# The S5 mixer of a two-block model rebuilt: five V products inside the first FFN, u and y turned by TensorE, y kept in PSUM with W stationary, the scan on one engine

## The chip, the cores and the metric

The kernel runs on one core of a Trainium2 chip. The metric is the device time of one execution in microseconds (us), as the median of several runs. A profiled execution of the same program gives the rows that are read below.

## What is computed

A model of 256 tokens and 1024 channels: a first block of four layers (mixers Fourier, S5, dilated attention, Fourier, each followed by a SwiGLU FFN) and a second block of two layers. Everything is float32. Only the S5 mixer, the mixer of layer 1, is touched. Cut to what matters, it is

```python
def _s5_direction(u, lam_re, lam_im, log_dt, b_re, b_im, c_re, c_im, reverse):
    lam = lax.complex(lam_re, lam_im)                    # 64 groups x 64 states
    dt = jnp.exp(log_dt)[:, None]
    lam_bar = jnp.exp(lam * dt)
    b_bar = ((lam_bar - 1.0) / lam)[..., None] * lax.complex(b_re, b_im)
    bu = lax.complex(einsum('bsgp,gnp->bsgn', u, b_bar.real),   # u: 256 tokens, 64 groups of 16 channels
                     einsum('bsgp,gnp->bsgn', u, b_bar.imag))
    # h[t] = lam_bar * h[t-1] + bu[t], forward or backward in time
    _, hs = lax.associative_scan(combine, (lam_bar, bu), axis=1, reverse=reverse)
    return einsum('gpn,bsgn->bsgp', lax.complex(c_re, c_im), hs).real

def s5_mixer(h, ...):
    y = (y_fwd + y_bwd).reshape(b, s, d) + d_skip * h
    g = jax.nn.gelu(y)
    val, gate = jnp.split(g @ w_glu, 2, axis=-1)
    return val * jax.nn.sigmoid(gate)
```

## The kernel before

The time axis of 256 tokens is cut into 32 chunks of 8 (S5_C = 32, S5_T = 8). The 64 groups are worked on in 8 tiles of 8 groups (f = 0..7). For each tile three factors are needed: **V** (powers of lam_bar times b_bar), which brings the inputs of a chunk into its state; **W** (powers of lam_bar times c), which brings the state carried into a chunk out to its 8 outputs; and a Toeplitz matrix of the **lags** inside a chunk. A V or a W is made elementwise by `s5_product`: 12 instructions of 128x512 elements on VectorE (DVE), or the same 12 on GpSimd (POOL).

Per tile, TensorE (PE) turns V (`factors`, 16 transposes), makes the lags from V and C (16 small matmuls), turns them (`toeplitz`, 8 transposes), applies V to u (L2049, "inputs", 32 matmuls into half of the output partitions each) and applies the Toeplitz matrix to u (L2057). ScalarE (ACT) copies each PSUM result out. V of tile 0 is made in the sixth chunk of the FFN before (`s5_first`); V of tiles 1 to 7 follow in the mixer, two buffers in turn.

u is wanted as rows (time in chunk, channel in group) by columns (tile, group, chunk), h is held as channels by tokens. Before, ACT permutes h (L957), ACT and POOL store it to DRAM in 8 DMAs (`s5_store_u`), and POOL loads it back in one. After the eight tiles the scan over 32 chunks runs as 30 steps of four dependent instructions, half of the columns on DVE (L1513 to L1518, 128x64), half on POOL (L790 to L793, 128x64). Then, per tile, PE multiplies the spread carried state (stationary) with W (moving) (`bring`, L2078), ACT copies the result (L1008), PE turns it back (`turn_back`, L2090), and DVE adds it to the y in SBUF (L1534). W of tiles 1 and 4 is made by POOL (`W_POOL`), the six others by DVE, four buffers in turn. y then takes the way of u through DRAM (`s5_store_y`, `s5_load_y`, two halves). Last come the skip term (L1541), GELU and the splitting into two float32r parts (L1023 to L1546), and the GLU projection of 8 weight panels (`project`, L1888 to L1890), each panel loaded by SP, split by ACT (L853) and DVE (L1324).

An FFN has 11 chunks of three weight panels each (`chunk`). PE's order in the FFN is fixed; DVE splits three panels per chunk (L1324) and makes the hidden activations (L1378 to L1393).

All engines run their own instruction list in order and meet through semaphores.

Of the kernel before, what the change touches and what calls it, by code (L numbers as in the profile page):

```python
# [12 lines left out]
P = 128  # L13
# [92 lines left out]
def build(nc, A, out, stop=None):  # L106
# [8 lines left out]
    with ExitStack() as ctx:  # L115
# [87 lines left out]
        s5_out_ready = sem("s5_out_ready")  # L203
        s5_y_ready = sem("s5_y_ready")
        s5_y_stored = {n: sem(f"s5_y_stored_{n}") for n in ("act0", "act1", "pool1")}
        s5_y_loaded = [sem(f"s5_y_loaded{i}") for i in range(2)]
        s5_cbd_ready = sem("s5_cbd_ready")
        s5_zbd_ready = sem("s5_zbd_ready")
        s5_wp_part = sem("s5_wp_part")
        s5_wp_ready = sem("s5_wp_ready")  # L210
        s5_skip_ready = sem("s5_skip_ready")
# [119 lines left out]
        s5.z = s5.take(2 * S5_G * S5_C).rearrange("p (r c k) -> p r c k", r=2, c=S5_G)  # L331
        s5.hperm = s5.z[:, 0].rearrange("p c k -> p (c k)").rearrange("p (f t c) -> p f t c", f=KT, t=S5_T)
        u_flat = s5.take(S5_G * S5_C)
        s5.u = u_flat.rearrange("p (g c) -> p g c", g=S5_G)
        s5.buf = [s5.take(2 * NC * P).rearrange("p (r c m) -> p r c m", r=2, c=NC) for _ in range(2)]
        win_flat = s5.take(2 * NC * P)
        s5.win = win_flat.rearrange("p (m q) -> p m q", m=2 * NC)
        b_flat = s5.take(2 * S5_G * S5_P)
        s5.b = b_flat.rearrange("p (r c m) -> p r c m", r=2, c=S5_G)
        s5.c = s5.take(2 * S5_G * S5_P).rearrange("p (r c m) -> p r c m", r=2, c=S5_G)  # L340
        s5.pow = s5.take(2 * (S5_T + 1) * S5_G).rearrange("p (r k c) -> p r k c", r=2, k=S5_T + 1)
        tmp_flat = s5.take(2 * NC * P)
        s5.tmp = tmp_flat[:, NC * P:].rearrange("p (r c m) -> p r c m", r=2, c=NC // 2)


        LAGS = 2 * S5_T - 1
        s5.kc = s5.take(LAGS * S5_P)

        s5.tc = rope[:, :, :].rearrange("p r s -> p (r s)").rearrange("p (g i m) -> p g i m", g=KT, i=S5_T)
        s5.rot = s5.take(2 * S5_G).rearrange("p (r c) -> p r c", r=2)  # L350
        s5.d = s5.take(KT)

        z_pool, z_dve = slice(0, S5_G // 2), slice(S5_G // 2, S5_G)
        s5.zp = s5.take(2 * S5_G).rearrange("p (i r c) -> p i r c", i=2, r=2)

        s5.back = [s5.take(2 * P)[0:2 * S5_C], s5.take(2 * P)[0:2 * S5_C], rstd[0:2 * S5_C, :]]
        s5_back_ready, s5_back_copied = s5_t_ready, s5_t_copied
        y_flat = hidden[:, :, :, :, :].rearrange("p a b t s -> p (a b t s)")
        s5.y = y_flat.rearrange("p (g c) -> p g c", g=S5_G)

        s5.w = s5.buf + [v.rearrange("p (r c m) -> p r c m", r=2, c=NC) for v in (win_flat, b_flat)]
        s5.wtmp = s5.tc.rearrange("p g i m -> p (g i m)").rearrange("p (r c m) -> p r c m", r=2, c=NC // 2)


# [2190 lines left out]
```

## Time and profile before

| what | us |
|---|---|
| median of 3 runs | 2757.31 (2755.21 to 2759.44) |
| profiled execution, its own time | 2759.11 |
| its span, first to last instruction | 2757.3 |
| PE busy over the span | 2598.0 (94%) |
| DVE busy | 1850.1 (67%) |
| ACT busy | 1265.1 (46%) |
| POOL busy | 308.6 (11%) |

The own time of the profiled execution is what compares with the median; its span leaves out what lies around the instructions. Stretches below are in us from the span's start. PE busy counts time, not pace; the clock in the rows is the granted TensorE clock as a share of full speed.

### The profile page before, as it was taken

The numbers are of one execution on the slowest core, as the hardware profiler recorded it, in microseconds if no ns is written. First come the engines' busy times: TensorE is split into PE (matmuls) and PEld (weight loads), VectorE is DVE, ScalarE is ACT, GpSimd is POOL, SyncE is SP. The second block draws the span as 40 slices with busy tenths as digits, with TensorE's granted clock in tenths as the row PEclk, the third lists the DMA queues.
The fourth block names the chain that finished last, engine by engine and source line by source line (L and its number), as shares of the span: only waits on it lengthen the run. The fifth ranks groups of instructions, "written<-read, shape, count | busy, mean of one in ns | idle before, by whom it ended". The sixth has DMA issues, their size and how long they took to land.

```text
span 2757.3 us, 51840 instructions
## 1 busy us (share of the span) xinstructions
PE 2598.0 (94%) x21706; PEld 2519.8 (91%) x21706; DVE 1850.1 (67%) x2303; ACT 1265.1 (46%) x1497; POOL 308.6 (11%) x419
## 2 busy tenths in 40 slices
PE   7997936999999999999999999999999999999998
PEld 7997835999899988999999999999999999999998
DVE  5765777655666575555657557986656656987655
ACT  5333413433455565334434334665434334665433
POOL 5400580000300010000000000230000000230000
PEclk9998967999999999999999999999999999999999
DMA  5554001555567773553554554444454554443553
GB/s 196 186 188 146 17 1 33 181 183 183 172 164 161 162 161 116 184 183 135 180 190 174 192 188 148 156 147 147 177 189 172 195 185 147 164 150 138 183 183 122
DMA packets 77781, 432.63 MB, mean 157 GB/s; under 512 B 20224, under 2 KB 23296, under 8 KB 27728
## 3 DMA queue, kind: packets, MB, share of 16 engines
q1 hardware_dynamic: 58720, 410.25, 41.4%
q0 software_dynamic: 5888, 17.53, 5.2%
q10 hardware_dynamic: 13040, 2.95, 0.6%
q8 instruction: 99, 1.62, 0.2%
q14 instruction: 34, 0.28, 0.0%
HBM read 426.40 MB, written 3.24 MB: 156 GB/s over the span
## 4 chain that ended last, share of the span: by engine, by line
PE 85%; DVE 8%; ACT 3%; POOL 1%; issue 1%; DMA 1%; ACTq 0%; DVEq 0%; POOLq 0%
PE psum L1888 25%; PE psum L1890 25%; PE psum L1889 25%; PE psum L2180 1%; DVE w_lo L1324 1%; PE psum L1921 1%; ACT w_hi L853 1%; PE psum L2156 1%; PE psum L2168 1%; PE psum L1990 1%; DVE arena L1513 1%; PE psum L2159 1%; DVE arena L1518 1%; DVE rstd L1349 1%; DVE h L1357 1%
## 5 line engine op out<-in xcount | busy, mean ns | idle before, releaser
L1888 PE MATMUL psum<-h_hi,w_hi 128*128 128x256 f32 x4320 | 1221.0, 283 | 32.4 <-DVE h_lo L1362 15.5
L1890 PE MATMUL psum<-h_hi,w_lo 128*128 128x256 f32 x4320 | 1211.5, 280 | 0.0
L1889 PE MATMUL psum<-h_lo,w_hi 128*128 128x256 f32 x4320 | 1211.2, 280 | 0.0
L853 ACT ACTIVATE w_hi<-raw 128x2048 fp32r<-128x2048 f32 x387 | 740.3, 1914 | 902.8 <-PE psum L1890 902.8
L1324 DVE TENSOR_TENSOR w_lo<-raw,w_hi 128x2048 fp32r<-128x2048 f32 x387 | 889.6, 2300 | 385.4 <-ACT w_hi L853 385.2
L1888 PEld LDWEIGHTS psum<-h_hi,w_hi 128*128 128x128 f32 x4320 | 815.1, 189 | 43.6 <-issue 35.7
L1889 PEld LDWEIGHTS psum<-h_lo,w_hi 128*128 128x128 f32 x4320 | 816.5, 189 | 1.2 <-issue 1.0
L1890 PEld LDWEIGHTS psum<-h_hi,w_lo 128*128 128x128 f32 x4320 | 815.5, 189 | 0.0
L1888 PE MATMUL psum<-act_hi,w_hi 128*128 128x256 f32 x1536 | 429.9, 280 | 1.7 <-DVE w_lo L1324 1.0
L1890 PE MATMUL psum<-act_hi,w_lo 128*128 128x256 f32 x1536 | 429.3, 280 | 0.0
L1889 PE MATMUL psum<-act_lo,w_hi 128*128 128x256 f32 x1536 | 429.1, 279 | 0.0
L1888 PEld LDWEIGHTS psum<-act_hi,w_hi 128*128 128x128 f32 x1536 | 288.0, 187 | 2.3 <-issue 1.2
L1889 PEld LDWEIGHTS psum<-act_lo,w_hi 128*128 128x128 f32 x1536 | 288.5, 188 | 0.0
L1890 PEld LDWEIGHTS psum<-act_hi,w_lo 128*128 128x128 f32 x1536 | 288.0, 187 | 0.0
L1386 DVE TENSOR_TENSOR hidden<-psum,rstd 128x512 f32<-128x512 f32 x88 | 60.8, 691 | 110.2 <-PE psum L1890 110.1
L1378 DVE TENSOR_TENSOR hidden<-psum,rstd 128x512 f32<-128x512 f32 x88 | 60.8, 691 | 103.6 <-PE psum L1890 103.3
L726 POOL DMA_DIRECT2D arena<-in_mix_col x2 | 1.2, 610 | 1106.4 <-DVE x L1423 1106.4
L1888 PE MATMUL psum<-w_hi,h_hi 128*128 128x256 f32 x320 | 92.2, 288 | 0.0
L1890 PE MATMUL psum<-w_hi,h_lo 128*128 128x256 f32 x320 | 89.7, 280 | 0.0
L1889 PE MATMUL psum<-w_lo,h_hi 128*128 128x256 f32 x320 | 89.4, 279 | 0.0
L2078 PE MATMUL psum<-arena 128*64 128x128 f32 x256 | 39.1, 319 | 51.5 <-DVE arena L1484 27.8
L1597 DVE SCALAR_TENSOR_TENSOR arena<-psum,arena 128x128 f32<-128x128 f32 (+1 forms) x96 | 32.0, 389 | 77.9 <-PE psum L2159 77.9
(313 smaller groups left out, 2689.7 us busy)
## 6 DMA issues: line engine op xcount, KB each, us to landing
raw<-in_panels SPq DMA_DIRECT2D x387, 1024.0 KB, 4.8
arena<-bias_by_distance POOLq DMA_DIRECT2D x32, 384.0 KB, 7.7
x<-in_x SPq DMA_DIRECT2D x1, 1024.0 KB, 7.4
arena<-in_s_b SPq DMA_DIRECT2D x1, 1024.0 KB, 15.0
arena<-in_s_c SPq DMA_DIRECT2D x1, 1024.0 KB, 16.5
arena<-s_u POOLq DMA_DIRECT2D x1, 1024.0 KB, 5.2
arena<-arena POOLq DMA_DIRECT2D x32, 32.0 KB, 1.9
out<-h SPq DMA_DIRECT2D x4, 256.0 KB, 2.2
```

Of the source, the lines that this page charges most:

```text
L853: a.activation(w_hi[:, s, :], raw[:, s, :], ACT.Copy).then_inc(hi_ready, 1)
L1324: v.tensor_tensor(w_lo[:, s, :], raw[:, s, :], w_hi[:, s, :].bitcast(F32), ALU.subtract).then_inc(lo_ready, 1)
L1349: v.reciprocal(rstd[:, :], rstd[:, :]).then_inc(rstd_ready, 1)
L1357: ins = v.scalar_tensor_tensor(h[:, c, :], x[:, c, :], gains[:, n * KT + c:n * KT + c + 1], rstd[:, :], ALU.mult, ALU.mult)
L1378: v.tensor_tensor(gate[:, c % 2], tiles(2 * c), rstd_2, ALU.mult).then_inc(scaled, 1)
L1386: v.tensor_tensor(act[:, b], tiles(2 * c + 1), rstd_2, ALU.mult).then_inc(scaled, 1)
L1513: v.tensor_tensor(m1, z0, l8, ALU.mult).then_inc(s5_step, 1)
L1597: ins = v.scalar_tensor_tensor(da.sc[:, u % 3, cols].rearrange("p (z j) -> p z j", j=P), da_bank(u)[:, cols].rearrange("p (z j) -> p z j", ...
L1888: t.matmul(o, w[0], xin[0], start=start, stop=False, skip_group_check=True)
L1889: t.matmul(o, w[0], xin[1], start=False, stop=False, skip_group_check=True)
L1890: return t.matmul(o, w[1], xin[0], start=False, stop=stop, skip_group_check=True)
L2078: last = t.matmul(bank[2 + n % 2][0:2 * S5_C, k * P:(k + 1) * P], s5.zbd[:, f % 2, r, 4 * d + pair, :], s5.w[f % 4][:, r, 4 * d + pair, :] ...
```

## The change

V of tiles 0 to 4 is made inside the FFN, a few instructions of it after each of its panels (8 per chunk from chunk 3 on, by a generator that `steps` draws from). The small block-diagonal form of C (`cbd`) is no longer made by POOL but computed on the host from the weights and loaded from HBM, 256 KB per tile. u is turned by PE: 128 matmuls of 32x32 tiles with a 0/1 matrix (`pick`) as weights, into PSUM, four copies out by ACT and DVE. The scan runs on DVE alone, all 128 columns in each instruction, and its tables and products lie in a PSUM bank. The Toeplitz product stays in PSUM, and the carried part is added to it there by PE, with W as the weights in 64x64 tiles and z moving (`carried`, 64 matmuls per tile of 31 columns). y is turned by 128 matmuls like those of u. POOL makes W of tiles 3, 4 and 5. The buffers are laid out anew: three of them are the slots of weight panels 37, 38 and 39, so that panels 39, 40 and 41 (the third, fourth and fifth of the GLU) are loaded only when the first carried tile, the last carried tile, and the turning of y are done. The order of the lag matmuls changes so that four neighbours write to four different column strips.

The diff, cut to its core:

```diff
-        W_POOL = (1, 4)
+        S5_EARLY = 5
+        W_POOL = (3, 4, 5)
+        W_DVE = (0, 1, 2, 6, 7)
+        W_ORDER = (0, 1, 2, 3, 4, 6, 5, 7)
+        def s5_bank(n):
+            return bank[4 + (n + 1) % 4]
+        def s5_y_bank(f, e):
+            return bank[f // 4 * 2 + e]
...
+                for n in range(s5_n0 + 2, s5_n0 + 5):
+                    sp.wait_ge(lo_ready, n - SLOTS + 1)
+                    if n == s5_n0 + 2:
+                        sp.wait_ge(s5_out_ready, W_ORDER.index(0) + 1)
+                    if n == s5_n0 + 3:
+                        sp.wait_ge(s5_out_ready, W_ORDER.index(7) + 1)
+                    if n == s5_n0 + 4:
+                        sp.wait_ge(s5_y_ready, 2)
+                    sp.dma_start(raw[:, n % SLOTS, :], A["panels"][n]).then_inc(panel_loaded[n % SLOTS], 16)
...
             def s5_mixer(st):      # GpSimd
+                for f in range(1, KT):
+                    if f >= 2:
+                        pool.wait_ge(s5_fill, s5_use("K", f - 2) + 1)
+                    pool.dma_start(s5.cbd[f % 2], A["s5_cbd"][f].rearrange("p (r c n) -> p r c n", r=2, c=NC)
+                                   ).then_inc(s5_cbd_loaded[f % 2], 16)
+                pool.wait_ge(s5_fill, s5_use("I", KT - 1) + 1)
...
                     split(p + 2, i, 6)
+                    steps(ahead, 3)
                     scale_gate(c, p, i)
                     split(p + 3, i, 6)
+                    steps(ahead, 2)
                     hidden(c, p, i)
                     split(p + 4, i, 6)
+                    steps(ahead, 3)
...
             def s5_mixer(st):      # VectorE
+                due = s5_v(5)
+                steps(due, 6)
+                v.wait_ge(s5_u_ready, 2)
+                for b in (1, 3):
+                    v.tensor_copy(s5.u[:, b].rearrange("p g f c -> p (g f c)"), bank[b][:, :]).then_inc(s5_u_copied, 1)
+                steps(due)
+                steps(s5_w(0))
+                for f in (6, 7):
+                    v.wait_ge(s5_fill, s5_use("K", f - 4) + 1)
+                    steps(s5_v(f))
+                for f, k in ((1, 4), (2, 5), (6, 6)):
+                    v.wait_ge(s5_fill, s5_use("K", k) + 1)
+                    steps(s5_w(f))
+                v.wait_ge(s5_evac, 64)
+                tabs = bank[5][:, 0:7 * S5_G].rearrange("p (i c) -> p i c", i=7)
                 for k in range(1, S5_C - 1):
-                    z0, z1 = s5.z[:, :, z_dve, k - 1], s5.z[:, :, z_dve, k]
+                    z0, z1 = s5.z[:, :, :, k - 1], s5.z[:, :, :, k]
...
+                steps(s5_w(7))
...
             def s5_mixer(st):      # TensorE
+                def rows_of_u(v):
+                    for g in range(2):
+                        for k in range(2):
+                            for b in range(4):
+                                rows = slice(b * 32, (b + 1) * 32)
+                                for tb in range(4):
+                                    i = S5_T - 1 - (2 * tb + k)
+                                    at = g * S + v * P
+                                    last = t.matmul(bank[b][tb * 32:(tb + 1) * 32, at:at + P],
+                                                    s5.pick[rows, g, (1 - k) * S5_P:(3 - k) * S5_P],
+                                                    h[rows, 4 * v:4 * v + 4, i::S5_T],
+                                                    start=(v + g + k == 0), stop=(v + g + k == 3), skip_group_check=True)
+                    last.then_inc(s5_u_ready, 1)
+                for f in range(KT):
+                    within(f)
+                    inputs(f)
+                    if f + 1 < KT:
+                        toeplitz(f + 1)
+                    if f + 2 < KT:
+                        factors(f + 2)
+                        lags(f + 2)
+                t.wait_ge(s5_step, 2 + 4 * (S5_C - 2))
+                for n, f in enumerate(W_ORDER):
+                    carried(f)
+                    if n == 5:
+                        channels_of_y(0)
+                channels_of_y(1)
```

Where the instructions go, at the three places that matter. First DVE in the FFN before the mixer, one chunk of its list. Here w_lo is the low part of a split panel, hidden the gate and up tiles, arena and rope the places of V and its temporaries. Before:

```order
L1324 TENSOR_TENSOR w_lo<-raw,w_hi 128x2048 [waits hi_ready] x2
L1378 TENSOR_TENSOR hidden<-psum,rstd 128x512 [waits panel_done]
L1324 TENSOR_TENSOR w_lo<-raw,w_hi 128x2048 [waits hi_ready]
L1386 TENSOR_TENSOR hidden<-psum,rstd 128x512 [waits panel_done]
L1389 TENSOR_TENSOR hidden<-hidden 128x512 [waits gate_ready,scaled]
```

And now, in chunks 3 to 10:

```order
L1271 TENSOR_TENSOR w_lo<-raw,w_hi 128x2048 [waits hi_ready]
L1434 TENSOR_TENSOR arena<-arena 128x512
L1436 TENSOR_TENSOR rope<-arena 128x512
L1438 TENSOR_TENSOR rope<-arena 128x512
L1325 TENSOR_TENSOR hidden<-psum,rstd 128x512 [waits panel_done]
L1271 TENSOR_TENSOR w_lo<-raw,w_hi 128x2048 [waits hi_ready]
L1441 TENSOR_TENSOR arena<-arena,rope 128x512 [waits s5_v_part]
L1443 TENSOR_TENSOR arena<-arena,rope 128x512
L1333 TENSOR_TENSOR hidden<-psum,rstd 128x512 [waits panel_done]
```

Up to three instructions of a product now stand between the split of a panel and the instruction that waits for PE.

Second, DVE's scan, one step of it before (the last row is the first of the next step):

```order
L1513 TENSOR_TENSOR arena<-arena 128x64 [waits s5_step]
L1514 TENSOR_TENSOR arena<-arena 128x64
L1516 TENSOR_TENSOR arena<-arena 128x2x32 [waits s5_step]
L1518 TENSOR_TENSOR arena<-arena 128x2x32 [waits s5_step]
L1513 TENSOR_TENSOR arena<-arena 128x64 [waits s5_step]
```

and now, with the two copies that fill the tables ahead of it:

```order
L1490 COPY psum<-arena 128x64 [waits s5_evac]
L1491 COPY psum<-arena 128x128
L1498 TENSOR_TENSOR psum<-arena,psum 128x128 [waits s5_step]
L1499 TENSOR_TENSOR psum<-arena,psum 128x128
L1501 TENSOR_TENSOR arena<-arena,psum 128x128 [waits s5_step]
L1503 TENSOR_TENSOR arena<-arena,psum 128x128 [waits s5_step]
```

The width doubles, and each instruction has one operand in PSUM where all were in SBUF.

Third, PE behind the scan. Before, one tile of eight (two halves, each brought out and turned back; arena holds the spread state, W and the copies):

```order
L2078 MATMUL psum<-arena 64x128 [waits s5_t_copied,s5_zbd_ready,s5_w_ready]
L2078 MATMUL psum<-arena 64x128 x7
L2090 MATMUL psum<-ident,arena 128x64 [waits s5_t_copied]
L2090 MATMUL psum<-ident,arena 128x64
L2078 MATMUL psum<-arena 64x128 [waits s5_t_copied]
```

Now two tiles of eight:

```order
L2063 MATMUL psum<-arena,raw 64x31 [waits s5_w_ready,s5_step]
L2063 MATMUL psum<-arena,raw 64x31 x63
L2063 MATMUL psum<-arena 64x31 [waits s5_w_ready]
L2063 MATMUL psum<-arena 64x31 x63
L2063 MATMUL psum<-arena 64x31 [waits s5_wp_ready]
```

Where a tile had 16 matmuls, two copies by ACT and four short matmuls, it now has 64 matmuls of 31 columns, one wait, and no copy between.

## Rows read from the trace of the kernel before

**Rows 1.** Busy us (count) of PE, PEld, DVE, ACT, POOL; clock, DMA share, GB/s.

```profile
216.00:250.40 34.40, 34.40 (x295) 34.40 (x294) 19.74 (x18) 14.33 (x11) 0.00 (x0) 1.00 0.53 183
250.40:280.60 30.20, 11.82 (x76) 9.42 (x74) 18.02 (x27) 11.00 (x20) 5.68 (x8) 0.66 0.46 105
280.60:362.90 82.30, 72.87 (x1032) 65.38 (x1032) 56.95 (x86) 32.77 (x64) 53.60 (x105) 0.94 0.01 2
362.90:422.40 59.50, 12.76 (x71) 11.64 (x70) 57.39 (x128) 6.68 (x17) 41.43 (x62) 0.61 0.00 0
422.40:460.70 38.30, 30.67 (x218) 26.73 (x218) 32.45 (x55) 12.27 (x32) 0.00 (x0) 0.89 0.11 14
460.70:480.70 20.00, 9.62 (x51) 9.32 (x51) 10.06 (x14) 8.70 (x15) 2.67 (x4) 0.66 0.35 79
```

**Rows 2.** The chain of waits, 255 to 283 us: start, us, what.

```profile
270.49 4.30 DMA s_u<-arena
...
275.36 5.17 DMA arena<-s_u
```

**Rows 3.** Timeline of PE, most of one of the eight tiles.

```profile
303.12 1.15 PE L2009 MATMUL psum<-ident,arena 128*128 128x128 f32 x8 [0.25 <-ACT arena L967]
304.19 2.46 PE L2021 MATMUL psum<-arena 128*32 128x128 f32 x32
306.58 1.97 PE L2057 MATMUL psum<-arena,rope 128*128 128x32 f32 x16
...
309.39 2.06 PE L2049 MATMUL psum<-arena 128*64 128x32 f32 x64
```

**Rows 4.** Timeline of DVE, the scan: first beside POOL, then alone.

```profile
386.40 1.11 DVE L1513 TENSOR_TENSOR arena<-arena 128x64 f32<-128x64 f32 x1
...
390.77 1.26 DVE L1513 TENSOR_TENSOR arena<-arena 128x64 f32<-128x64 f32 x1
...
393.77 0.26 DVE L1513 TENSOR_TENSOR arena<-arena 128x64 f32<-128x64 f32 x1
...
394.12 0.26 DVE L1516 TENSOR_TENSOR arena<-arena 128x64 f32<-128x64 f32 x1
394.41 0.27 DVE L1518 TENSOR_TENSOR arena<-arena 128x64 f32<-128x64 f32 x1
```

**Rows 5.** Timeline of POOL, a W product beside that scan.

```profile
383.76 1.26 POOL L812 TENSOR_TENSOR arena<-arena,rope 128x512 f32<-128x512 f32 x1
```

**Rows 6.** Timeline of PE, half a tile brought out.

```profile
434.91 1.96 PE L2078 MATMUL psum<-arena 128*64 128x128 f32 x16
```

**Rows 7.** Timeline of DVE, part of a chunk of the FFN.

```profile
216.65 0.69 DVE L1378 TENSOR_TENSOR hidden<-psum,rstd 128x512 f32<-128x512 f32 x1 [1.41 <-PE psum L1890]
218.59 2.29 DVE L1324 TENSOR_TENSOR w_lo<-raw,w_hi 128x2048 fp32r<-128x2048 f32 x1 [1.25 <-ACT w_hi L853]
...
229.90 2.29 DVE L1324 TENSOR_TENSOR w_lo<-raw,w_hi 128x2048 fp32r<-128x2048 f32 x1 [2.79 <-ACT w_hi L853]
```

**Rows 8.** Timeline of PE, the sums of the norm ahead of the mixer.

```profile
250.37 3.62 PE L1921 MATMUL psum<-h,ones 128*128 128x256 f32 x16
```

**Rows 9.** Timeline of DVE, the eight instructions that make h.

```profile
256.38 3.25 DVE L1357 SCALAR_TENSOR_TENSOR h<-x,gains,rstd 128x256 f32<-128x256 f32 x8
```

**Rows 10.** Timeline of DVE, instructions with one operand in PSUM.

```profile
29.15 0.29 DVE L1456 TENSOR_TENSOR h<-h,psum 128x127 f32<-128x127 f32 x1 [1.89 <-ACT h L923]
29.36 0.28 DVE L1457 TENSOR_TENSOR h<-h,psum 128x127 f32<-128x127 f32 x1
...
45.48 0.68 DVE L1438 TENSOR_TENSOR x<-psum,x 128x512 f32<-128x512 f32 x1
```

**Rows 11.** Timeline of POOL at the same time.

```profile
45.67 0.60 POOL L669 TENSOR_TENSOR arena<-arena 128x64 f32<-128x64 f32 x2
```

**Rows 12.** The page, DMA issues: KB of each, median us from issue to landing.

```profile
raw<-in_panels SPq DMA_DIRECT2D x387, 1024.0 KB, 4.8
...
x<-in_x SPq DMA_DIRECT2D x1, 1024.0 KB, 7.4
```

More of the change, by code:

```diff
@@ L329, in take @@
                 return arena[:, cls.at - n:cls.at]
[L331 to L337, printed above, removed]
@@ L356, in build @@
[L356 to L362, printed above, removed]
@@ new lines, in toeplitz, with inputs @@
+                def toeplitz(f):
+                    t.wait_ge(s5_evac, s5_use("K", f) + 1)
+                    for q in range(2):
+                        to = take(s5_use("C", f) + q)
+                        for i in range(4):
+                            last = t.transpose(to[:, i * P:(i + 1) * P],
+                                               s5.kc[:, (4 * q + i) * S5_P:(4 * q + i) * S5_P + P], ident[:, :])
+                        last.then_inc(s5_fill, 1)
+                def inputs(f):
+                    t.wait_ge(s5_evac, s5_use("T", f) + 4)
+                    to = take(s5_use("I", f))
@@ L2053, in s5_mixer @@
-                    t.wait_ge(s5_t_copied, 2 * f + 2)
-                    if f:
-                        t.wait_ge(s5_intra_copied, f)
-                    for g in range(KT):
-                        last = t.matmul(bank[1][:, g * S5_C:(g + 1) * S5_C], s5.tc[:, g].rearrange("p i m -> p (i m)"),
-                                        s5.u[:, f * KT + g, :], start=True, stop=True)
-                    last.then_inc(s5_intra_ready, 1)
-                w_dve = [f for f in range(KT) if f not in W_POOL]
@@ L2095, in s5_mixer @@
-                for n in range(2 * KT):
-                    bring(n)
-                    if n:
-                        turn_back(n - 1)
-                turn_back(2 * KT - 1)
+                                rhs = s5.u[:, c % 4, e, f, :] if c < 4 else s5.u[:, c % 4, e, f, ::-1]
+                                last = t.matmul(to[half[e], (r * NC + c) * S5_C:(r * NC + c + 1) * S5_C],
+                                                s5.win[f % 2][:, r * NC + c, half[e]], rhs, start=True, stop=True)
@@ new lines, in s5_mixer @@
+                factors(0)
+                lags(0)
+                toeplitz(0)
+                factors(1)
+                lags(1)
+                t.wait_ge(s5_loaded, 64)
+                for v in range(2):
+                    t.wait_ge(h_ready, 4 * st["whole"] + 2 * v + 2)
+                    rows_of_u(v)
+                t.wait_ge(s5_u_copied, 4)
+                for f in range(KT):
+                    within(f)
+                    inputs(f)
+                    if f + 1 < KT:
+                        toeplitz(f + 1)
+                    if f + 2 < KT:
+                        factors(f + 2)
+                        lags(f + 2)
```

508 lines of the change are left out of this document (231 added, 277 removed).

## The prediction

> **What bounds the kernel now.** I read the page first, then the busy time by stretch, then the chain of waits and the timelines inside the mixer. Outside the mixer PE runs nearly without a gap, so the change can only win or lose inside it and in the FFN ahead. In the mixer no single engine bounds; four stretches follow one another [rows 1]. From 250.4 to 280.6 us (30.2 us) PE is busy 11.8 us: the norm, then u on its way through DRAM, whose last two legs alone are 4.30 and 5.17 us [rows 2]. From 280.6 to 362.9 (82.3 us) PE is busy 72.9 us and sets the pace in most tiles: V turned, lags, Toeplitz, inputs [rows 3]. From 362.9 to 422.4 (59.5 us) PE has 12.8 us of work at a mean clock of 0.61 and waits for the scan and the first W products; DVE is busy 57.4. From 422.4 to 460.7 (38.3 us) DVE's W products pace PE. From 460.7 to 480.7 (20.0 us) y goes through DRAM and PE does the first GLU panel, much of it at the slow clock (mean 0.66). The FFN before them passes 295 matmuls in 34.4 us, 0.117 us each at full clock.
>
> The scan deserves a look [rows 4]. Alone, a step of four DVE instructions takes 0.94 us (393.77 to 394.41, plus 0.30 for the last). Beside POOL's W products it takes 4.37 us (386.40 to 390.77): each DVE instruction lasts 1.11 to 1.26 us, and a POOL instruction beside them 1.26 [rows 5]. DVE's instructions there have two inputs in SBUF.
>
> **The change part by part.** I carry the new clock along, from 250.4, and compare at the same events.
>
> *V in the FFN.* Four more products of 12 instructions of 128x512, at 0.69 us each (the row of such an instruction [rows 7]), are 4 x 12 x 0.69 = 33 us of DVE. In a chunk DVE idles 1.41, 1.25 and 2.79 us at three of its waits [rows 7]; a fourth is like the first. The eight instructions per chunk (5.5 us) go in as three, two and three. Three are 2.1 us against 1.41: the gate product starts 0.7 us late. What is late next is ACT's silu, which stands behind ACT's split of the next panel, and DVE waits 1.25 us for that split anyway, so the 0.7 us ends there. Price 0; with that cover gone, 0.7 us in each of eight chunks, 5 us; at the very most all 33 us.
>
> *The start of the mixer.* The norm's sums end at 250.4 + 3.6 = 254.0 [rows 8]. PE then turns V0 and V1, makes two sets of lags and one Toeplitz without waiting for h: transposes 4 x 1.15 + 1.1 us, lags 2 x 1.0 (below), so 7.8 us with a stop for a copy: 261.8. h is complete at 259.6 [rows 9]. Turning u is 128 matmuls, each two records in the trace. Inputs at 32 columns in two column strips pass at 2.06/64 = 32 ns, start to start 31 ns per record [rows 3]. A 128-column record in one strip alone is 1.96/16 = 122 ns, less its tail 109 [rows 6]. With four strips in turn I take 31 ns, the smallest spacing any row shows: 256 x 31 = 8.0 us. Bounds: a quarter of 109, 27 ns, is 7 us; no overlap, 109 ns, is 28 us. Then 1.4 us of copies by two engines: the tile loop begins at 271.2 where it began at 280.6. **Minus 9.4.**
>
> *The tile loop.* Inputs 2.0, within-chunk 1.9, transposes 2.1 and 0.9 stay. Lags, 32 records in 2.4 us, 75 ns each where one strip is used eight times running [rows 3], now go round four strips: 31 ns, 1.0 us. Bound: unchanged 2.4, which is 8 x 1.4 = 11 us more in all. Six rounds of 8.1, and 9.7 for the last two tiles with one wait for a copy: 58.3 us. DVE has V5, V6, V7 and W0, W1, W2, W6 to make, 6.5 x 12 x 0.69 = 54 us from 271 on (half of V5 is made earlier), done with the loop's last tile, some 4 us before its end; POOL no longer spreads C (PE waited 7.7 us for that). The loads of C, 256 KB each, start two rounds ahead. With the last copy the scan starts at 330.3.
>
> *The scan.* 30 steps of 128 columns. PSUM instructions of 127 columns last 0.28 to 0.29 us and follow each other at 0.21 [rows 10]. A step is two at 0.21 to 0.25 and two dependent ones at 0.32 to 0.37 (duration plus the 0.03 to 0.04 that the lone scan shows [rows 4]): 1.06 to 1.24 us, I take 1.12. 33.6 us plus 0.7 for the tables: **364.6**. This supposes that POOL no longer holds DVE up, though it makes W3, W4, W5 just then (12 instructions of 1.1 to 1.26 us [rows 4, 5], 13.8 us each, 41 us). For it: at 45.48 a DVE instruction with one input in PSUM took its usual 0.68 us while POOL worked from 45.67 on [rows 10, 11]. That is one instruction beside narrow POOL ones. The Trainium skill, "SBUF — State Buffer", section on who interferes with whom, makes it a rule: a DVE instruction with at most one SBUF input does not contend with GpSimd, one with two does. By it the scan is the same 33.6 us. If it did contend, nine steps of 4.37 would pass in 41 us and 21 more of 1.12: 63 us, 30 more. Loop and scan together: 93.4 us where 82.3 + 59.5 = 141.8 stood. **Minus 48.4.**
>
> *Out of the scan.* PE sat idle over 30 us, so it starts at the 1.2 GHz level (clock 0.5); in the last stretch before, 51 matmuls were busy 9.6 us where 0.117 each makes 6.0, 3.6 us lost over two starts [rows 1]; I take 2.1 for one. Carried: 8 x 128 records x 31 ns = 32 us. Bounds: two of these 64x64 tiles at a time is what the 31 ns shows; four at a time would be 15.5 ns, 16 us; one at a time 58 ns (two at a time is 2 x 29), 59 us. I take the row. Turning y: 8 us, as for u (7 to 28). Copies between: 0.9. 43.0 us against 38.3: y is turned at 407.6. **Plus 4.7.** Before, such a tile took two halves of 1.96 us plus the turning back, about 4.4 us [rows 6], mostly hidden behind DVE; now 4.0 of PE. The Trainium skill, "TensorE: Matmul & The Clock Gate", section "Wait — 56ns, not 53.3ns?", says that matmuls never start closer than about 25 ns however few columns they have, which speaks against W as weights with 31 columns moving: more and smaller matmuls gain nothing. An estimate by it: 8 x 128 x 25 ns = 25.6 us for the carried part, 6 us under my row; it rules out the 16.
>
> W3 and W4 are due when three and four tiles are done, W5 as the seventh; POOL has them at about 343, 357 and 371. W7 follows the scan on DVE, 8 to 10 us. No wait.
>
> *The end.* One DVE round of additions 1.5 us, the low part of b = 0 another 0.7, then 48 matmuls of 0.117, 5.6 us at full clock, GELU of the second half hidden behind the first parts: 7.9 us against 20.0. **Minus 12.1.** Panels 39, 40, 41 are waited for by SP: 39 is free early, 40 after the last carried tile, 41 after the turning; a panel lands 4.8 us after issue [rows 12], and they are wanted 14 us and more behind the turning. Nothing late.
>
> *The start of the kernel.* 256 KB more beside the 1024 KB of x, which lands after 7.4 us [rows 12]: at most a quarter of that, 1.9 us, if it all shared x's way; it is issued after three loads on another queue, so I take 0.5.
>
> **The sum.** -9.4 - 48.4 + 4.7 - 12.1 + 0.5 = -64.7. The profiled execution took 2759.1 us in all (span 2757.3), the median is 2757.3; both lose the same, so 2757.3 - 64.7 = **2692.6 us**.
>
> **The rivals.**
> - *PE is faster in tiles.* 16 to 26 us carried, lags and turning at 27 ns: 8 to 18 us less, 2675 to 2685. For it: four disjoint tiles follow each other. Against: no row shows it.
> - *POOL still stops the scan*: plus 30, 2723. For it: the 4.37 us steps. Against: [rows 10, 11].
> - *PE's tiles overlap only in part*: the 32x32 turns at 60 to 109 ns (plus 15 to 40), or carried at 58 ns (plus 27): 2706 to 2745. For it: h is read with a stride of 8 elements, which no row shows.
> - *The FFN is held up* by the products, which are not hidden: up to plus 33, 2726.
> - *Slower than before: no overlap at all.* Turns plus 20 each, lags plus 11, carried plus 27: plus 78, 2771, 0.5% slower. It decides from 65 us on, that is when the mean record costs about 85% of these surcharges. Against: the inputs' 31 ns in two strips is overlap.
> - *The change does not do what it says*: the stall of the scan only moves behind W3 to W5. It would need POOL to take 20 us per product; it takes 13.8.
>
> **How the numbers follow.** Forecast (2685 to 2706) 0.5; faster PE 0.2; partial overlap 0.13; POOL contention 0.06; FFN held up 0.05; no overlap 0.03; something that eats the gain 0.03. The range reaches over the faster case's middle and most of the partial ones: 2670 to 2728. A measurement of this kernel tells 0.2% (5.5 us) from no change. Faster 0.95, same 0.01, slower 0.04.
>
> **What would show it.** In the changed profile: the FFN's chunks still 17 us and PE without gaps there; u turned in 8 us from about 262; rounds of 8 us with lags of 1.0; scan steps of 1.12 us that do not change when POOL ends; records of the carried part 31 ns apart; 8 us from the last turn to the end of the first GLU panel. I am wrong if scan steps are over 2 us, if 128 turning matmuls take over 15 us, or if PE waits for w_lo in the FFN.

## The result, and the profile after

The changed kernel takes 2696.53 us (median of four runs, 2688.91 to 2698.23), the kernel before on the same chips 2756.26 us: a ratio of 0.9776, 95% interval 0.9755 to 0.9797, 60 us less. The prediction said 2692.6 us, 2670 to 2728.

The profiled execution took 2698.23 us (span 2696.4) where that of before took 2759.11: 60.9 us less, against 64.7 predicted. Busy time by stretch answers to [rows 1], in the same columns (PE, PEld, DVE, ACT, POOL, clock, DMA):

```profile
214.00:248.00 34.00, 34.00 (x291) 34.00 (x290) 25.81 (x28) 14.42 (x11) 0.00 (x0) 1.00 0.34 121
251.50:266.30 14.80, 12.49 (x360) 9.71 (x358) 10.03 (x18) 7.38 (x15) 1.10 (x2) 1.00 0.14 39
266.30:328.50 62.20, 60.38 (x984) 57.13 (x984) 49.57 (x80) 27.11 (x54) 3.15 (x5) 0.90 0.07 19
328.50:370.80 42.30, 0.00 (x0) 0.00 (x0) 40.23 (x121) 4.26 (x9) 39.79 (x36) 0.50 0.00 0
370.80:408.80 38.00, 34.83 (x1280) 32.30 (x1280) 10.51 (x17) 3.98 (x7) 0.00 (x0) 0.50 0.17 54
408.80:420.50 11.70, 8.78 (x51) 8.81 (x52) 7.04 (x9) 4.22 (x6) 0.00 (x0) 0.61 0.41 147
```

The FFN's stretch has PE busy all 34.00 us, five products or one; busy time says nothing of pace, but 291 matmuls in 34.0 us is the pace of before (295 in 34.4). From the end of the norm's sums to the start of the 48th matmul of the first GLU panel it is 168.6 us where it was 226.3. The third stretch ends with the scan's first step: all of the scan, 42.3 us, lies bare, with PE idle. The last three stretches run at half clock or little more.

The timeline of PE, from the norm's sums into the tile loop, answers to [rows 8] and [rows 3]:

```profile
251.33 1.91 PE L1991 MATMUL psum<-ident,arena 128*128 128x128 f32 x16
253.17 1.08 PE L2003 MATMUL psum<-arena 128*32 128x128 f32 x32
...
258.52 3.92 PE L2045 MATMUL psum<-h,arena 32*32 32x128 f32 x174
262.81 2.04 PE L2045 MATMUL psum<-h,arena 32*32 32x128 f32 x82 [0.37 <-issue]
266.33 2.38 PE L2033 MATMUL psum<-raw,hidden 128*128 128x32 f32 x16 [1.48 <-DVE raw L1474]
268.65 3.63 PE L2024 MATMUL psum<-raw,arena 128*64 128x32 f32 x64
272.21 1.97 PE L2013 MATMUL psum<-ident,arena 128*128 128x128 f32 x8
...
277.11 1.97 PE L2033 MATMUL psum<-raw,hidden 128*128 128x32 f32 x16
279.01 2.06 PE L2024 MATMUL psum<-raw 128*64 128x32 f32 x64
281.00 1.09 PE L2013 MATMUL psum<-ident,arena 128*128 128x128 f32 x8
```

Lags take 1.08 us where they took 2.46. Turning u is the 256 records of L2045: 6.3 us, 25 ns each. Behind it stands one wait, 1.48 us for the copy. A round is 7.67 us (277.11 to 284.78); the first has the same instructions longer, at the slow clock.

The scan answers to [rows 4], and POOL beside it to [rows 5]:

```profile
356.71 0.38 DVE L1498 TENSOR_TENSOR psum<-arena,psum 128x128 f32<-128x128 f32 x1
357.00 0.37 DVE L1499 TENSOR_TENSOR psum<-arena,psum 128x128 f32<-128x128 f32 x1
357.28 0.38 DVE L1501 TENSOR_TENSOR arena<-arena,psum 128x128 f32<-128x128 f32 x1
357.70 0.40 DVE L1503 TENSOR_TENSOR arena<-arena,psum 128x128 f32<-128x128 f32 x1
358.13 0.38 DVE L1498 TENSOR_TENSOR psum<-arena,psum 128x128 f32<-128x128 f32 x1
```

```profile
357.46 1.11 POOL L781 TENSOR_TENSOR hidden<-arena 128x512 f32<-128x512 f32 x1
```

A step is 358.13 - 356.71 = 1.42 us with POOL at work right beside it; all 30, before and after POOL's last instruction at 369 us, take 42.3.

PE behind the scan, and into the first GLU panel:

```profile
370.85 3.64 PE L2063 MATMUL psum<-arena,raw 64*64 64x31 f32 x128 [43.40 <-DVE arena L1503]
374.28 5.53 PE L2063 MATMUL psum<-arena 64*64 64x31 f32 x199
381.21 12.38 PE L2063 MATMUL psum<-arena 64*64 64x31 f32 x441 [1.40 <-issue]
393.53 3.54 PE L2077 MATMUL psum<-raw,arena 32*32 32x128 f32 x128
...
405.89 2.82 PE L2077 MATMUL psum<-raw,arena 32*32 32x128 f32 x128 [0.81 <-DVE raw L1511]
411.72 0.55 PE L1865 MATMUL psum<-h_hi,w_hi 128*128 128x256 f32 x1 [3.01 <-DVE h_lo L1523]
412.07 0.41 PE L1866 MATMUL psum<-h_lo,w_hi 128*128 128x256 f32 x1
412.29 0.41 PE L1867 MATMUL psum<-h_hi,w_lo 128*128 128x256 f32 x1
```

Carried records stand 12.38/441 = 28 ns apart, at the slow clock, with pauses marked "issue", in which PE waits for nothing that the profile shows (1.40 us). Behind the last turning PE idles 3.01 us for h's low part, and the panel starts at 0.21 us a matmul.

### The profile page after: what moved, and what is told of

Read it like the earlier page. It is cut to its first block, busy times and chain, and to the rows that moved or that the text cites. A ratio compares the mean times of both kernels' runs of the same rounds, so it can differ in the third digit from the quotient of the medians.

```text
span 2696.4 us, 54054 instructions
## 1 busy us (share of the span) xinstructions
PE 2579.1 (96%) x22954; PEld 2507.2 (93%) x22954; DVE 1822.7 (68%) x2288; ACT 1242.6 (46%) x1442; POOL 241.6 (9%) x276
## 4 chain that ended last, share of the span: by engine, by line
PE 90%; DVE 6%; ACT 2%; issue 1%; DMA 0%; DVEq 0%; ACTq 0%
PE psum L1865 26%; PE psum L1866 26%; PE psum L1867 25%; PE psum L2187 1%; PE psum L2063 1%; DVE w_lo L1271 1%; PE psum L1898 1%; ACT w_hi L818 1%; PE psum L2163 1%; PE psum L2175 1%; PE psum L2024 1%; PE psum L1967 1%; PE psum L2033 1%; PE psum L1991 1%; PE psum L2166 1%
## 5 line engine op out<-in xcount | busy, mean ns | idle before, releaser
L1865 PE MATMUL psum<-h_hi,w_hi 128*128 128x256 f32 x4320 | 1220.7, 283 | 24.7 <-DVE h_lo L1309 14.9
L1098 ACT ACTIVATE arena<-psum 128x512 f32<-128x512 f32 x48 | 28.6, 597 | 96.2 <-PE psum L1867 95.9
## 6 DMA issues: line engine op xcount, KB each, us to landing
arena<-in_s_b SPq DMA_DIRECT2D x1, 1024.0 KB, 15.4
```

The costliest lines, as they stand in the source:

```text
L1098: a.activation(dst, halves(landed(p)), func).then_inc(mix_copied, 1)
L1865: t.matmul(o, w[0], xin[0], start=start, stop=False, skip_group_check=True)
```

## The experiments

All start from the changed kernel unless said otherwise; changed_again is that kernel unedited, run beside shared_early. Times are medians (two_tiles_in_turn ran once); ratios are to the kernel before on the same chip. The table reads each profile's PE timeline: "sums" is where the norm's sums end, then come the stretches in us: to the start of the tile loop; from there to the first carried record (loop and scan); to the last turning; to the start of the 48th matmul of the first GLU panel; and their sum.

| kernel | median | sums | start | loop, scan | out | end | sum |
|---|---|---|---|---|---|---|---|
| changed | 2696.5 | 251.5 | 14.8 | 104.5 | 37.9 | 11.4 | 168.6 |
| changed_again | 2697.7 | 251.4 | 15.4 | 105.1 | 38.0 | 10.9 | 169.3 |
| scan_in_sbuf | 2722.8 | 252.7 | 15.5 | 130.0 | 39.0 | 10.1 | 194.6 |
| w_all_dve | 2700.7 | 251.4 | 15.3 | 105.2 | 38.2 | 10.5 | 169.2 |
| early_one | 2723.6 | 246.6 | 41.7 | 105.8 | 37.2 | 11.3 | 196.0 |
| same_tile_runs | 2734.4 | 244.6 | 42.3 | 115.2 | 37.4 | 10.9 | 205.8 |
| two_tiles_in_turn | 2715.2 | 251.4 | 24.6 | 105.7 | 38.2 | 10.9 | 179.5 |
| warm_pe | 2699.1 | 250.9 | 15.4 | 105.9 | 35.3 | 8.9 | 165.5 |
| early_lo | 2695.9 | 245.3 | 15.5 | 105.6 | 38.3 | 7.3 | 166.7 |
| shared_scan | 2691.3 | 253.3 | 15.5 | 94.3 | 38.6 | 11.0 | 159.3 |
| shared_early | 2679.8 | 245.0 | 15.5 | 93.5 | 39.0 | 7.4 | 155.5 |
| shared_early_warm | 2685.6 | 244.3 | 15.4 | 95.1 | 35.8 | 7.3 | 153.6 |

The sums end anywhere from 244.3 to 253.3 us with the same instructions ahead of them (early_one's apart): some executions passed the dense matmuls of the first FFN almost 3% faster (1092 in the 125 us from 120 in early_lo, 1064 in the changed kernel and in the kernel before), all at a granted clock of 1.00. So a difference of 3 us is read from the stretch, not from the median.

**Does the scan's place free it from POOL?** scan_in_sbuf puts the tables and products back into SBUF:

```
-tabs = bank[5][:, 0:7 * S5_G].rearrange(...)
+tabs = hidden_flat[:, 1024:1024 + 7 * S5_G].rearrange(...)
```

> The changed kernel with one line moved: the scan's tables and products lie in SBUF instead of a PSUM bank, so that every scan instruction has two SBUF inputs again, beside the same POOL products. Theory 1 (the operands' place is what freed the scan from POOL): beside POOL's 36 instructions DVE instructions wait for POOL's as in the kernel before (1.11 to 1.26 us each, 4.37 us a step), so nine or ten steps pass in POOL's 41 us, and the other 20 at 1.2 to 1.4 us: the scan takes 41 + 26 = 67 us instead of 42.3, the kernel about 25 us more than the changed one, 2721 us. Theory 2 (POOL and DVE did not meet because of timing or width, not because of the place): the scan takes 42 us or less, and the kernel 2690 to 2697 us.

2722.8 us, ratio 0.988 (0.9847 to 0.9912): 26 us more than the changed kernel. The timelines of DVE and of POOL, in the scan:

```profile
345.37 1.19 DVE L1499 TENSOR_TENSOR hidden<-arena,hidden 128x128 f32<-128x128 f32 x1
346.48 0.38 DVE L1501 TENSOR_TENSOR arena<-arena,hidden 128x128 f32<-128x128 f32 x1
346.89 1.27 DVE L1503 TENSOR_TENSOR arena<-arena,hidden 128x128 f32<-128x128 f32 x1
```

```profile
345.25 1.15 POOL L782 TENSOR_TENSOR hidden<-arena 128x512 f32<-128x512 f32 x1
346.48 1.44 POOL L784 TENSOR_TENSOR arena<-arena,hidden 128x512 f32<-128x512 f32 x1
```

From 330 to 371 us DVE got 44 instructions through, from 371 to 398 us 76. The scan took 69.7 us (theory 1 said 67). Theory 2 falls. The rule of the Trainium skill, "SBUF — State Buffer", section "Who interferes with whom", holds here: two SBUF inputs contend, one does not.

**The same part alone in the kernel before.** before_psum_scan moves only DVE's half of the scan (64 columns) to PSUM:

```
-l8, rot = s5.pow[:, 0, S5_T, z_dve]..., s5.rot[:, :, z_dve]
-m1, m2 = (tmp_flat[:, i * S5_G:(i + 1) * S5_G]...)
+tabs = bank[0][:, 0:7 * S5_G // 2]...  # copies of both tables, m1, m2
```

> The kernel before with one part of the change alone: DVE's half of the scan (64 columns) keeps its tables and products in a PSUM bank. POOL's half of the scan and its W products stay. Theory 1: no step waits for POOL any more; 30 steps of 0.94 to 1.1 us from 361.7 us on end at about 393 instead of 414.7 us. Of these 21 us PE gets back what the later W products don't take: 12 to 20 us, the kernel 2757 - 15 = 2742 us. Theory 2: POOL's instructions hold up the scan wherever its operands lie; no change, 2757 us.

2747.78 us, ratio 0.9951 (0.9932 to 0.9969): 13.5 us less by the ratio, 12.4 by the medians. The scan's steps are 0.93 us and it ends at 389.97 us; in the kernel before DVE's first product behind it starts at 414.71:

```profile
414.71 0.69 DVE L1478 TENSOR_TENSOR arena<-arena 128x512 f32<-128x512 f32 x1
```

The scan ends 24.7 us earlier, then, but only about half of it arrives. Here is where the rest went, DVE's next products and POOL's W4 beside them:

```profile
402.42 1.48 DVE L1478 TENSOR_TENSOR arena<-arena 128x512 f32<-128x512 f32 x1
403.82 1.74 DVE L1479 TENSOR_TENSOR arena<-arena 128x512 f32<-128x512 f32 x1
405.49 1.75 DVE L1480 TENSOR_TENSOR arena<-arena 128x512 f32<-128x512 f32 x1
```

```profile
398.79 1.55 POOL L808 TENSOR_TENSOR arena<-arena 128x512 f32<-128x512 f32 x1
```

Products with two SBUF inputs now meet POOL's: 1.5 to 1.75 us each instead of 0.69, and POOL's 1.4 to 1.7 instead of 1.1 to 1.3. The stall moved one stage on.

**What a step costs by itself.** w_all_dve has the scan in SBUF and POOL silent:

```
-W_POOL = (3, 4, 5)
-W_ORDER = (0, 1, 2, 3, 4, 6, 5, 7)
+W_POOL = ()
+W_ORDER = (0, 1, 2, 6, 3, 7, 4, 5)  # DVE makes 3, 7, 4, 5 behind the scan
...
-tabs = bank[5][:, 0:7 * S5_G].rearrange(...)
+tabs = hidden_flat[:, 1024:1024 + 7 * S5_G].rearrange(...)
```

> The changed kernel with the scan's tables and products in SBUF and with POOL silent: W3, W4, W5 and W7 are made by DVE after the scan (8.3 us each), and the tiles are taken in the order 0, 1, 2, 6, 3, 7, 4, 5. It sizes a step of 128 columns with SBUF operands and nothing beside it. If PSUM costs time by itself: 1.1 to 1.25 us a step (four instructions at 0.94 for 64 columns, and 64 columns more each), the scan 35 us instead of 42.3. If only the 64 columns more cost it: 1.41 us a step, 42 us. Behind the scan DVE's 33 us of products pace the tiles: W5 is there 33 us after the scan's end, PE is done with the last tile 37 us after it, then 8 us of turning and copies less: 4 us more than the changed kernel there. Together 2694 us in the first case, 2701 us in the second.

2700.7 us. DVE's timeline, a step from SBUF alone:

```profile
345.98 0.40 DVE L1503 TENSOR_TENSOR arena<-arena,hidden 128x128 f32<-128x128 f32 x1
346.41 0.37 DVE L1498 TENSOR_TENSOR hidden<-arena,hidden 128x128 f32<-128x128 f32 x1
346.69 0.35 DVE L1499 TENSOR_TENSOR hidden<-arena,hidden 128x128 f32<-128x128 f32 x1
346.97 0.39 DVE L1501 TENSOR_TENSOR arena<-arena,hidden 128x128 f32<-128x128 f32 x1
347.39 0.40 DVE L1503 TENSOR_TENSOR arena<-arena,hidden 128x128 f32<-128x128 f32 x1
```

347.39 - 345.98 = 1.41 us, as from PSUM. With 64 columns it was 0.94 from SBUF [rows 4] and 0.93 from PSUM. So PSUM costs this scan nothing; the 64 columns more cost 0.47 us a step. Four DVE products behind the scan cost PE nothing either (38.2 against 37.9, where the expectation had 4 us more): POOL's share was not needed there.

**What the early V products are worth.** early_one sets S5_EARLY to 1 and makes V1 to V4 at the head of the mixer.

```
-S5_EARLY = 5
+S5_EARLY = 1
+for f in range(S5_EARLY, 5): steps(s5_v(f))   # head of the mixer
```

> The changed kernel with one V product inside the FFN, as before, and V1 to V4 at the head of the mixer. My account: DVE makes 4 x 8.3 = 33 us of products from 251.5 us on, so the copies of u come at 289 us instead of 266, and the tile loop and all behind it 22 us later: 2719 us; the FFN is as long as before, so its chunks are not faster without them. Rival: the products did hold up the FFN, and its chunks give 5 us back: 2714 us.

2723.6 us, ratio 0.9884 (0.9848 to 0.9921). The start grows from 14.8 to 41.7 us, 27 us for 31 us of products (252.21 to 283.10 on DVE); the rest stays. The FFN gives nothing back, and the products in it were free: PE passes the same 1064 matmuls from 120 to 245 us in the kernel before, with one product, as in the changed kernel, with five; and early_one, one of the faster executions, ends its sums at 246.6 us where those with five products end theirs at 244.3 to 245.3 (1097 matmuls against 1091 or 1092 from 120 to 245 us, 0.7 us of them at most). The expectation of 22 us let the products start with the end of the sums. They start 5.6 us behind it, once h is made; the 4.10 us that DVE idled ahead of the copies of u in the changed kernel is what makes 27 of 31.

**Does the order of PE's tiles matter?** same_tile_runs changes lags back to four matmuls per row strip and turns u with four matmuls per 32x32 tile; two_tiles_in_turn turns u with two tiles in turn:

```
-for g in range(2): for k in range(2): for b in range(4): for tb in range(4):
+for b in range(4): for tb in range(4): for g in range(2): for k in range(2):   # same_tile_runs
+for b in range(4): for pair in range(2): for g ...: for k ...: for tb in pair:  # two_tiles_in_turn
```

> The changed kernel with the order of the small matmuls changed back in two places: lags take the four of one row strip in succession (as in the kernel before), and turning u takes the four of one 32x32 tile in succession. Same instructions, same count. My account (matmuls in disjoint tiles of PE overlap, those in the same tile do not): lags 2.4 us instead of 1.05, eight times, of which the tile loop pays six to eight: 8 to 11 us; turning u at 75 ns a record 19 us instead of 6.2, 13 us; together 21 to 24 us more, 2719 us. Rival: the spacing is set by the issue of instructions, whatever tile they go to: 2697 us.

> The changed kernel with turning u in another order: two 32x32 tiles of PE in turn instead of four. With one tile the 256 records took 31.1 us (121 ns each, at a mean clock of 0.59), with four 6.3 us (24 to 25 ns, clock 1.00). If a record occupies its own tile and tiles work side by side, two tiles in turn give half of one tile's spacing: 38 ns each at the full clock (the lags of one strip take 75), 60 at the slow one, 10 to 15 us for all. If only a direct repeat of the same tile costs something, two in turn take 6.3 us as four do.

2734.4 us (ratio 0.9912, 0.989 to 0.9934) and 2715.2 us. PE's timeline of same_tile_runs:

```profile
251.92 2.46 PE L2003 MATMUL psum<-arena,hidden 128*32 128x128 f32 x32
254.31 31.07 PE L2045 MATMUL psum<-h,arena 32*32 32x128 f32 x256
```

One tile: 121 ns a record; two in turn 63 (16.1 us for 256); four 25. Lags 2.46 us again, 10.7 us in loop and scan. Issue does not set the spacing, and two tiles in turn take half of one tile's: the tiles work side by side. Neighbours here differ in the strip of output partitions too, so whether a repeat waits for the tile or for its strip of PSUM is not shown. My 19 us missed that the clock falls as well: its mean was 0.59 in those 31 us, 0.68 with two tiles, 1.00 with four. The Trainium skill, "TensorEngine Tiling (Array Packing)", section "Key Properties", has the rule that different tiles run in parallel; the three spacings agree.

**What the slow clock costs behind the scan.** warm_pe adds matmuls of zeros that nobody reads:

```
+for k in range(S5_C - 2 - 14, S5_C - 2):
+    t.wait_ge(s5_step, 2 + 4 * k)
+    dummy(bank[6], 5 if k < S5_C - 4 else 2)
...
 channels_of_y(1)
+dummy(bank[3], 7)
```

> The changed kernel with added matmuls of zeros into banks that nobody reads: five of 128x512 after each of the scan's last 14 steps (two in the last), and seven behind the last turning of y, where PE stood idle 3.0 us. It asks what the granted clock of 0.50 costs behind the scan. Theory A (PE falls to the slow level in its 43 us of idle time and small tiles don't bring it back): it stands at 1.00 when the carried part begins, falls back during it, and only the dense matmuls ahead of the first GLU panel count: 1 to 2 us less than the changed kernel, 2695 us. Theory B (small tiles hold a clock that is already high): 1.00 up to the end, the first GLU panel in 5.6 us instead of 8.7, 3 to 4 us less, 2693 us. Theory C (the carried records are bound by columns at the slow clock, 31 columns in 28 ns): the carried part itself gets shorter, 28.5 us down to 20 us, 2684 us. In any case the scan stays at 1.41 us a step.

2699.1 us, ratio 0.9781 (0.9763 to 0.9798): no gain in the time, 3.1 us in the stretch. Its windows:

```profile
372.20:380.00 7.80, 6.99 (x360) 6.89 (x361) 7.58 (x12) 0.00 (x0) 0.00 (x0) 0.78 0.38 139
380.00:386.00 6.00, 3.64 (x175) 3.41 (x168) 0.00 (x0) 0.84 (x2) 0.00 (x0) 0.77 0.01 3
386.00:407.50 21.50, 20.06 (x762) 18.25 (x761) 2.89 (x5) 3.14 (x6) 0.00 (x0) 0.50 0.12 41
407.50:416.80 9.30, 9.22 (x61) 8.11 (x58) 7.11 (x9) 4.22 (x5) 0.00 (x0) 0.84 0.39 144
```

```profile
375.11 2.72 PE L2063 MATMUL psum<-arena 64*64 64x31 f32 x135
378.60 2.06 PE L2063 MATMUL psum<-arena 64*64 64x31 f32 x128 [0.77 <-issue]
382.34 2.97 PE L2063 MATMUL psum<-arena 64*64 64x31 f32 x128 [1.67 <-issue]
```

Carried records stood 16 ns apart while the granted clock was 1.00 (2.06/128), and 20 over a stretch in which it rose (2.72/135, mean clock 0.77), instead of 28. But the pauses marked issue grew, from 2.0 us to 3.6 in all, and the clock did not stay: finer windows have it at 0.50 from 373 us, at 1.00 again from 376 to 383, and at 0.50 from 384 us on. Theory C was right on the records and wrong on the sum, and theory A was right that the clock falls back: out of the scan PE gained 2.6 us, not 8.

**The wait ahead of the GLU.** early_lo makes the low parts of the first four tiles of h ahead of the second half's additions:

```
 v.tensor_copy(s5.y[:, 1, 1]..., s5_y_bank(4, 1)[:, :])
+lower((0, 1))
...
-for b in range(4): ...
+lower((2, 3))
```

> The changed kernel with one change of order on DVE: the low parts of the first four tiles of h come before the additions of the second half of y, not behind them. PE then need not wait 3.0 us for them after the last turning and begins the first GLU panel there. The clock is at its slow level either way and rises as long after the panel's start as before. 2.9 us less than the changed kernel: 2693.6 us. Rival: the low parts come too late themselves, since ACT makes their GELU only after its copy of y, and push the additions back: no gain, 2697 us.

2695.9 us, ratio 0.9777 (0.976 to 0.9793). PE starts the panel at once:

```profile
401.89 2.82 PE L2082 MATMUL psum<-raw,arena 32*32 32x128 f32 x128 [0.81 <-DVE raw L1518]
404.64 0.58 PE L1870 MATMUL psum<-h_hi,w_hi 128*128 128x256 f32 x1
```

The end takes 7.3 us instead of 11.4. The whole stretch is 1.9 to 2.6 us shorter than in the two profiles of the changed kernel; the expected 2.9 us do not show in the median, which is 0.7 us less.

**Sharing the scan again, without contention.** shared_scan gives POOL, which then makes no W product, the columns of tiles 0 to 3, beside DVE's products in the loop, and DVE the others from PSUM, with W3, W7, W4 and W5 behind its scan; shared_early adds early_lo, shared_early_warm zeros during the scan as well:

```
+pool.wait_ge(s5_evac, s5_use("I", KT // 2 - 1) + 1)
+for k in range(1, S5_C - 1): ...   # as DVE's four instructions, columns 0 to 31
-z0, z1 = s5.z[:, :, :, k - 1], s5.z[:, :, :, k]
+z0, z1 = s5.z[:, :, z_dve, k - 1], s5.z[:, :, z_dve, k]
```

> The changed kernel with the scan cut in two by columns: POOL takes the 64 columns of tiles 0 to 3 as soon as they are there (about 298 us), DVE the other 64 after the loop with its tables in PSUM; POOL makes no W product, DVE makes W3, W7, W4, W5 behind its scan, tiles in the order 0, 1, 2, 6, 3, 7, 4, 5. DVE's scan takes 30 x 0.94 = 28.2 us instead of 42.3. POOL's 30 steps took 1.62 us alone and about twice that beside DVE's products in the kernel before: 50 to 60 us, from 298 us to 348 or 358 us, in time for DVE's end at 357 us. DVE's products in the loop take 0.83 us instead of 0.69 beside POOL; DVE has 10.6 us to spare there. Behind the scan the tiles are paced as in the run with all W on DVE (41.2 us to the first GLU panel, against 40.9). Forecast: 14 us less than the changed kernel, 2683 us. Rival: the contention holds up V6 and V7, the loop gets 5 us longer and POOL's scan ends last: 2690 to 2697 us.

> The changed kernel once more, unedited, on the chip of the two runs beside it. Expected: 2693 to 2699 us, and 168 to 169 us from the end of the norm's sums to the 48th matmul of the first GLU panel, wherever on the clock the sums end (in the runs so far between 244.6 and 253.3 us, with the same instructions ahead of them).

> The scan shared between POOL and DVE (as in the run shared_scan, 159.3 us from the end of the norm's sums to the 48th matmul of the first GLU panel, against 168.6 in the changed kernel) together with the low parts made ahead of the second half's additions (1.9 to 2.9 us). The two touch different stretches, so the savings should add: 156 to 157 us in that stretch, 11 to 12 us less than the changed kernel of the same call, 2685 us. If instead something at the end of the chain takes the early low parts' gain back, 159 us and 2688.

> The same, with matmuls of zeros on PE: four of 128x512 behind each of DVE's last 14 scan steps and ten more until POOL's part of the scan ends. PE then begins the carried part at the full level. In the run warm_pe the carried part and the turning took 35.3 us instead of 37.9 and the clock was back at 0.5 by 380 to 386 us. Expected: 2 to 3 us less than without the zeros, 153.5 to 154.5 us in the stretch, 2682.5 us. Rival: the pauses for instructions between the small matmuls, which grew in warm_pe from 1.8 to 4.3 us in all, take it back: no gain.

shared_scan: 2691.3 us, ratio 0.9748 (0.9732 to 0.9765). DVE's scan ends at 359.7 us but POOL's at 363.0, and PE starts then: loop and scan 94.3 us, 10 us less, not 14. POOL starts only at 305.2 us, behind its last load of C, for which it waits on PE 7.12 us, where the expectation had 298. Its 30 steps take 57.8 us, inside the expected 50 to 60: 0.68 to 0.80 us an instruction beside DVE's products, 0.35 alone and, from 331 to 359 us, beside DVE's scan from PSUM. With the early low parts, beside changed_again on one chip: 2679.8 us (expected 2685), ratio 0.9709 (0.9695 to 0.9722), against 0.9763 (0.9747 to 0.9779) for the changed kernel beside it. This version beats both kernels, the changed one by 0.6%. With zeros as well the stretch is 1.9 us shorter, yet the median is 2685.6 (0.9735, 0.9721 to 0.9748), higher than without (expected 2682.5). Its profile is the fastest of its five executions (2676.3 to 2689.5 us) and has the faster pace in the FFN; of the others no row shows the pace, so why the median is higher stays open.

Two parts of the change no run puts back: the way of u and y through DRAM, and W as the moving operand with its copies. What they are worth is read from the stretches alone.

## Why the prediction was right

The sum was 3.8 us too hopeful for the profiled execution (60.9 against 64.7), out of terms that were off by up to 9 us and partly cancelled. That it came so near is in part luck. In the rebuilt stretch alone it promised 65.2 us (9.4 + 48.4 - 4.7 + 12.1) and got 57.7 (226.3 - 168.6), 7.5 too few. Of these 3.0 came back ahead of the stretch, where the sums ended 2.5 us earlier instead of 0.5 later, for no reason that the change gives, and 0.7 behind it.

- *V in the FFN, price 0.* Right: the FFN's pace is that of before (1064 matmuls in 125 us), and early_one gets nothing back.
- *Start, -9.4.* -11.8. Turning u took 6.3 us, not 8.0: 25 ns a record, under the 31 ns of two strips. same_tile_runs shows that the order bought it.
- *Tile loop, 59.8 us to the scan's first step.* 62.2. Rounds of 7.7 us are better than the 8.1 forecast; the rounds at a clock of 0.65 and 0.73 (the first and third) cost more than that:

```profile
266.30:276.10 9.80, 9.77 (x105) 9.47 (x105) 9.59 (x16) 3.00 (x6) 0.00 (x0) 0.65 0.01 2
276.10:286.70 10.60, 10.60 (x187) 9.91 (x186) 10.32 (x17) 5.22 (x11) 1.10 (x2) 1.00 0.11 29
286.70:293.00 6.30, 6.30 (x89) 6.10 (x88) 6.20 (x11) 2.96 (x6) 0.00 (x0) 0.73 0.11 39
```

- *The scan, 33.6 us.* 42.3: the one large mis-sized term, 8.7 us. "PSUM instructions of 127 columns last 0.28 to 0.29 us" was taken as the price of 128 columns; here they last 0.37 to 0.40. w_all_dve shows that it is not PSUM. The contiguous operations in [rows 10] do not stand for a scan that reads every 32nd element of z; whether it is that stride is open, no run changed it. That POOL does not hold it up was right, and scan_in_sbuf shows the reason.
- *Out of the scan, 43.0 us.* 37.9: 28 ns a record, not 31, even at the slow clock, and turning y 6.4 us, not 8. The 2.1 us for the clock came as slow clock throughout, and pauses of 2.0 us had no term. The estimate from the Trainium skill's 25 ns ("TensorE: Matmul & The Clock Gate", section "Wait — 56ns, not 53.3ns?"; 25.6 us for the carried part) was about as near to the 29 us that it was busy as my 32. But I let it rule out 16 ns a record, and that was wrong: in warm_pe records stood 16 ns apart at a clock of 1.00. A matmul is two records, so 32 ns; what kept the carried part from 16 us was the clock and the pauses, not this floor.
- *The end, 7.9 us.* 11.7: I had PE at full clock there. It had been at 0.50 all through the small tiles and idled 3.01 us; most of the panel's matmuls passed at 0.21 us.
- *Start of the kernel, +0.5.* x landed after 5.9 us, not 7.4, and the sums ended 2.5 us earlier. By the spread of that point between executions this is no effect of the change.

Of the rivals, "PE is faster in tiles" came in part (some 6 us: 1.7 and 1.6 in the two turnings, 2.5 in the carried part), and the clock and the scan took it back. "POOL still stops the scan" and "no overlap" are what scan_in_sbuf (26 us) and same_tile_runs (37 us) show when their causes are put back; the prices in the prediction were 30 and, for the same two places (one turning, lags), 31.

## What to carry to other kernels

Two engines that share SBUF are costed by what each instruction reads: moving one operand of a short dependent chain to PSUM took the stall away at no price per step, but the stall goes to the next instructions with two SBUF inputs if the other engine is still at work then. Small matmuls are ordered so that neighbours use different tiles of PE; the same 128 matmuls took 6.3, 16.1 or 31.1 us by nothing but their order, with the mean clock at 1.00, 0.68 and 0.59. A stage that was rebuilt leaves a new bare stretch (here a scan of 42 us with PE idle): look for work that can start earlier, and size a chain by rows with its own access pattern.

## What the runs showed of the hardware

- Two records of the trace stand for each small matmul. Carried records were 28 ns apart at a granted clock of 0.50 and 16 ns at 1.00 (warm_pe, 2.06/128). Turning does not follow the clock so: u took 25 ns a record at 1.00, the second half of y 22 ns (2.82/128) at 0.50.
- In the changed kernel PE stayed at the 1.2 GHz level through 34.83 us of 64x64 and 32x32 tiles in 38.00, and rose only within the dense GLU panel behind them. In warm_pe it fell from 2.4 GHz at 373 us, when it had been busy 0.88 of the 2 us from 370 on, rose at 376 while it passed 64x64 tiles without a gap, fell at 383.6 behind pauses (3.64 us busy in the 6.00 from 380), and stayed down through 20.06 busy us in 21.50. So the level rose within such tiles in one run and not in the other; what decides is open.
- A train of small matmuls is interrupted by pauses that no semaphore explains: 2.0 us in the 38 us out of the scan, 3.6 us in warm_pe and 5.0 in shared_early_warm, where the train ran faster at first (the expectation of shared_early_warm counts 1.8 and 4.3 for the first two). Counted from the first carried record, they stand behind 327, 967 and 1095 records in the changed kernel, behind 263, 391, 519 and 903 in warm_pe, behind 261, 389, 517 and 901 in shared_early_warm: within every run whole multiples of 128 records apart, and elsewhere when matmuls of zeros are put ahead. So they hang on the place in PE's instruction list and not on the data. That PE waits for its own instructions is likely, not shown.
- Dense matmuls at the same granted clock of 1.00 passed at two paces, 117.5 and 114.5 ns each, from execution to execution; this moved the end of the norm's sums from about 251 to about 245 us. The 253.3 of shared_scan has the slower pace, and 860 matmuls instead of 875 in the first 120 us; why is open.
- A POOL instruction of 128x64 took 0.35 us alone and beside DVE's scan from PSUM, 0.68 to 0.80 beside DVE's products with two SBUF inputs (shared_scan).
